# The last SwiGLU products of a feed-forward block are rounded into the end of another buffer

## What is computed

```python
def swiglu(x, w_gate, w_up, w_down):
    return (jax.nn.silu(x @ w_gate) * (x @ w_up)) @ w_down

h = h + 0.5 * swiglu(rmsnorm(h, ffn_norm_a[i]), ffn_a_w_gate[i], ffn_a_w_up[i], ffn_a_w_down[i])
m = rmsnorm(h, mix_norm[i])          # then the mixer, then a second such block
```

## Time and profile before

| | us |
|---|---|
| median of 3 executions | 1533.07 (1533.01 to 1557.75) |
| the profiled execution | 1533.33 |
| its span | 1531.5 |

### The profile page before, as it was taken

One profiled execution on the slowest core, in us unless ns is written; L12 is line 12 of the kernel. 1 busy time (PEld: TensorE's weight loads), 2 busy tenths in 40 slices (PEclk: granted clock), 3 DMA queues, 4 the chain that ended last, 5 costly groups with the idle time before them and its releaser, 6 DMA issues.

```text
span 1531.5 us, 24245 instructions
## 1 busy us (share of the span) xinstructions
PE 1448.1 (95%) x9470; PEld 1325.2 (87%) x9470; DVE 941.3 (61%) x1344; ACT 740.0 (48%) x1004; POOL 48.2 (3%) x88
## 2 busy tenths in 40 slices
PE   7999978899988999988999999999998999999997
PEld 7899978899987888888898888788887999888886
DVE  5545676655555665657756666666667369666655
ACT  5546553143435544435744544544444438554443
POOL 1000000000000000000010000100000000000000
PEclk9999989999999999979999999999999999999999
DMA  8342420155543555534156455475654410455552
GB/s 309 138 157 95 167 98 28 56 182 189 187 142 134 188 200 192 168 132 152 45 193 219 168 202 189 159 247 169 209 190 146 166 56 2 138 178 189 195 192 82
DMA packets 33907, 239.11 MB, mean 156 GB/s; under 512 B 3946, under 2 KB 4090, under 8 KB 5808
## 3 DMA queue, kind: packets, MB, share of 16 engines
q1 hardware_dynamic: 32544, 232.02, 43.9%
q0 software_dynamic: 1296, 6.15, 1.2%
HBM read 237.07 MB, written 1.08 MB: 156 GB/s over the span
## 4 chain that ended last, share of the span: by engine, by line
PE 79%; DVE 2%; ACT 1%; issue 1%; POOL 0%; POOLq 0%; DVEq 0%; ACTq 0%
PE ps L669 20%; PE ps L640 12%; PE ps L641 12%; PE ps L642 12%; PE ps L672 10%; PE ps L771 2%; PE ps L794 2%; PE ps L781 1%; PE ps L998 1%; PE ps L2191 1%; PE ps L2199 1%; PE ps L2203 1%; PE ps L582 1%; PE ps L2317 1%; PE ps L992 0%
## 5 line engine op out<-in xcount | busy, mean ns | idle before, releaser
L380 DVE TENSOR_TENSOR low<-raw,high 128x2048 fp32r<-128x2048 f32 (+1 forms) x193 | 437.8, 2268 | 252.5 <-ACT high L374 252.0
L374 ACT ACTIVATE high<-raw 128x2048 fp32r<-128x2048 f32 (+1 forms) x193 | 364.4, 1888 | 61.9 <-PE ps L642 56.5
L669 PE MATMUL ps<-nt,high 128*128 128x512 f32 x1344 | 335.8, 392 | 0.0
L669 PEld LDWEIGHTS ps<-nt,high 128*128 128x128 f32 x1344 | 244.2, 189 | 46.3 <-issue 0.9
L640 PE MATMUL ps<-nt,high 128*128 128x256 f32 x736 | 212.3, 288 | 6.4 <-DVE nt L471 5.5
L641 PE MATMUL ps<-nt,high 128*128 128x256 f32 x736 | 210.6, 286 | 0.0
L642 PE MATMUL ps<-nt,low 128*128 128x256 f32 x736 | 210.5, 286 | 0.0
L672 PEld LDWEIGHTS ps<-nt,low 128*128 128x128 f32 x1344 | 183.3, 190 | 13.1
L672 PE MATMUL ps<-nt,low 128*128 128x256 f32 x1344 | 187.4, 282 | 0.0
L640 PEld LDWEIGHTS ps<-nt,high 128*128 128x128 f32 x736 | 143.7, 195 | 7.9 <-DVE low L380 4.4
L640 PE MATMUL ps<-high,hth 128*128 128x512 f32 x352 | 138.0, 392 | 6.1 <-DVE htl L1173 6.1
(11 more groups left out here) (341 smaller groups left out, 2189.5 us busy)
## 6 DMA issues: line engine op xcount, KB each, us to landing
raw<-in_stream SPq DMA_DIRECT2D x217, 1024.0 KB, 4.9
late<-in_w POOLq DMA_DIRECT2D x1, 2048.0 KB, 8.7
scr<-bias_by_distance POOLq DMA_DIRECT2D x1, 2048.0 KB, 13.3
scr<-in_mem SPq DMA_DIRECT2D x2, 512.0 KB, 4.8
x<-in_x SPq DMA_DIRECT2D x1, 1024.0 KB, 8.8
out<-xs SPq DMA_DIRECT2D x2, 512.0 KB, 2.6
row<-in_row SPq DMA_DIRECT2D x1, 588.0 KB, 10.5
con<-in_con SPq DMA_DIRECT2D x1, 577.0 KB, 9.8
```

The lines of the kernel that those rows point to most:

```text
L374: nc.scalar.activation(high[t % SLOTS][:, 0:n], raw[t % SLOTS][:, 0:n], ACT.Copy).then_inc(w_high, 1)
L380: nc.vector.tensor_tensor(low[t % SLOTS][:, 0:n], raw[t % SLOTS][:, 0:n], high[t % SLOTS][:, 0:n].bitcast(F32), ALU.subtract).then_inc(w_l ...
L669: nc.tensor.matmul(r3(bank, 2), wt[0][:, k, col:col + P], nt[:, :, k, :], start=k == 0, stop=False, skip_group_check=True)
```

## The change

The high and low products of the last column of a block (c = 10) go into the last two chunks of `nth` and `ntl`, not into `hth` and `htl`. `last_down` reads them there. Since nobody reads these chunks any more, the rounding waits for the products alone and no longer for the ninth `down`. On ACT and DVE the last iteration of the loop is written out behind the loop, which now has eight; PE's loop keeps nine. In the written-out iteration the split of tile tb + 33 stands behind the rounding on ACT, and its low half behind the subtraction on DVE; before, both stood ahead of them.

```diff
+        hth_last, htl_last = nth[:, KC - 2:KC, :], ntl[:, KC - 2:KC, :]
@@ last_down
-                                             [h[:, j, P * tt:P * tt + P] for h in (hth, htl)],
+                                             [h[:, j, P * tt:P * tt + P] for h in (hth_last, htl_last)],
@@ act_ffn
-            with act.Fori(0, FT - 2) as i:
+            with act.Fori(0, FT - 3) as i:
                 split_high(act, tb + 7, i)
 ...
                 rounded(tb + 7, n0 + 2, i)
+            te, ne = tb + 3 * FT - 4, n0 + FT - 1
+            split_high(act, te + 2)
+            gate_cross(te, ne)
+            gated(ne)
+            split_high(act, te + 3)
+            up_cross(te + 1, ne)
+            act.wait_ge(ff_h, ne + 1)
+            nc.scalar.activation(hth_last, r3(ff["h"], 2), ACT.Copy).then_inc(ff_hhigh, 1)
+            split_high(act, te + 4)
@@ dve_ffn
-            with dve.Fori(0, FT - 2) as i:
+            with dve.Fori(0, FT - 3) as i:
                 split_low(dve, tb + 7, i)
 ...
                 rest(n0 + 2, i)
+            te, ne = tb + 3 * FT - 4, n0 + FT - 1
+            split_low(dve, te + 2)
+            gate_sum(ne)
+            gate_norm(ne)
+            split_low(dve, te + 3)
+            up_sum(ne)
+            hidden(ne)
+            dve.wait_ge(ff_hhigh, ne + 1)
+            nc.vector.tensor_tensor(htl_last, r3(ff["h"], 2), hth_last.bitcast(F32), ALU.subtract).then_inc(ff_hlow, 1)
+            split_low(dve, te + 4)
```

## The result

| | before | after |
|---|---|---|
| median of 6 executions each, us | 1533.23 (1533.01 to 1557.75) | 1556.23 (1555.75 to 1557.21) |
| ratio of the times, 95% interval | | 1.015 [1.0136, 1.0164] |
| span of the profiled execution, us | 1531.5 | 1554.4 |
| mean granted clock | 0.977 | 0.960 |

The kernel became slower by 23 us, where 1.4 us less was forecast and 1535.2 was the upper end. Each execution of either kernel is at one of two levels, about 24 us apart, and the ratio compares different ones: five of before at the lower, without its sixth at 1557.75, with all six of after at the upper.

What follows compares the result with a forecast made beforehand. PE was taken to bound the kernel, carrying 79% of the chain. Terms 0.37 + 0.42 + 0.64 - 1.8 + 1.77 gave 1.4 us less, 1531.7 us for the median, range 1529.3 to 1535.2.

Steps and rivals of the forecast that it cites:

- The rounding: End of each block: the low half is ready 1.1 us early, so PE saves 1.77 us if nothing else is late.
- Rival 4: The rounding is not in time, so the change does nothing: 1533.3 us; chance 0.04.
- DVE is late next; updates gain 0.42: Block ends: DVE must split two tiles before updating x, so updates, and block 1 with them, gain only 0.42 us.
- Blocks 0 and 2 gain 0.64: Norms behind these blocks: the second square follows the first directly, a gain of 0.64 us passed on to the turns.
- Idle stretches of 3.8 us: Behind blocks 0 and 2, PE's idle stretch ahead of the norm's turns grows from 2.48 to 3.8 us.
- The clock falls behind block 2, for 6.8 us, price 1.8: Behind block 2 the longer idle stretch brings half clock for 6.8 us, losing 1.8 us in turns and first products.
- Block 0, "0.37, if it comes back at the same moment": Behind block 0 the 0.64 us lead falls at half clock, worth 0.37 us if full clock returns at the same moment.
- the sum: Whole kernel: the gains and losses of blocks 0 to 3 and block 2's clock fall together give 1.4 us less.
- Rival 3: Block 0's half clock goes away because its stretch begins elsewhere: about 1525 us; chance 0.08.
- Rival 2: Half clock behind block 2 lasts long; at 17.0 us, 3.0 us slower, 1536.1; chance 0.17, mostly below 1535.

Runs made afterwards that it cites:

- late_low: The changed kernel with DVE's low half of tile +34 moved behind the updates and turned inputs: 1523.84 to 1525.16 us at full clock, 4 of 10 at half clock.
- after_again: The changed kernel run once more, nothing altered, beside before: ratio 0.9981 at full clock, 3 of 10 executions at half clock.
- before_late_norm: The kernel before, with ACT's first square of the norm behind block 0 made twice: ratio 1.0004, 10 of 10 at full clock.
- before_shift2: The kernel before, with two unused matmuls ahead of the first down of block 0: 1 of 10 at half clock, the others at ratio 1.0006.
- before_fill_all: The kernel before, with unused matmuls behind blocks 0 and 2, ahead of the latent inputs' turns and ahead of the attention's scores: 1530.5 us, ratio 0.9977.

## Why the prediction was right or wrong

Step by step, by distances from the last matmul of `up` of a block (L672), start to start, in the two traces:

- **The rounding.** Right. Block 3, where nothing is late next, ends 1.78 us earlier (end of its last product, 12.97 to 11.19); 1.77 was forecast. Rival 4 is out.
- **DVE is late next; updates gain 0.42.** Right: 0.45 in block 1 (first turn 11.26 to 10.81), and the new wait of 1.66 us for 1.5 forecast. late_low shows the cause: with the low half of +34 gone from ahead of the updates, the same distance is 8.99, another 1.8 us.
- **Blocks 0 and 2 gain 0.64.** Wrong by 0.2: the first turns come 0.46 and 0.45 earlier (15.47 to 15.01, 15.48 to 15.03). The second square did move as forecast (1187.85, right behind the first, 1.06 after it), but what follows did not gain by it: POOL's next step (L526) takes 0.65 us where it took 0.41, the one behind it (L529) starts 3.0 us after the first square in both kernels, and the second turns of block 2 stand 1.47 us behind the first in both.
- **Idle stretches of 3.8 us.** Right: 3.82 and 3.84.
- **The clock falls behind block 2, for 6.8 us, price 1.8.** Right in this trace. The fall is there and lasts 6.8 us (1190.48 to 1197.30). The first product comes 0.20 us closer behind `up` than before (19.32 to 19.12), but the products behind it are slower: the 41st stands 24.32 us behind `up` before (1175.50) and 25.53 after (1200.22), and all later ones keep this 1.21. With 0.45 gained ahead of the turns the fall costs 1.66, and block 2 loses 1.21 where the forecast, 0.64 less 1.8, was a loss of 1.16. How long the fall lasts is of the execution: in after_again it lies at 1165.39, lasts 3.4 us, and block 2 loses only 0.04 in all.
- **Block 0, "0.37, if it comes back at the same moment".** The condition failed. The half clock behind block 0 lasted 17.1 us before (663.55 to 680.62) and 20.5 after (661.41 to 681.89): it began 2.1 us earlier and ended 1.3 later. The first score came 0.7 us *later*, not 0.4 earlier (732.02 for 731.30), 0.51 of it behind block 0's last `up`. In after_again the half clock was 17.1 us again (663.63 to 680.69), with the same program, and the first score stood 0.17 closer behind `up` than before. So the moment of the fall belongs to the execution, not only to the kernel.
- **The places of the edit together.** In the trace of after they give -0.51 + 0.45 - 1.21 + 1.78 = 0.5 us less, for the 1.4 of the sum. The other side, 23.2 us more, is none of them.
- **The failing step** is a stage that the sum put at nothing: the attention behind block 0. The prediction followed the clock where the edit makes PE's idle stretches longer, behind blocks 0 and 2, and stopped there. The stretch of 2.16 us ahead of the attention is the same before and after, so it entered neither the sum, nor a rival, nor the range. Yet it is followed by a fall, and the work behind it can stay at half clock for 54.6 us. Rival 3's argument, that "all executions shown (1533.01, 1533.07 and the profiled 1533.33) agree too well for a fall that comes and goes", left out the fourth number in the table, 1557.75. That was by its time this very state, 24.7 us above the median (no trace of that execution was kept), and it said both that something in this kernel comes and goes and what it costs.
- **Rivals.** Rival 2 had the right sign and the right kind of mechanism at the wrong place: a half clock that lasts long. Its worst case, 17 us of products, was taken as the longest because the one trace showed none longer.

The Trainium skill, page "TensorE: Matmul & The Clock Gate", Part 1 (The HAM clock gate), says that the gate runs freely and does not restart with the kernel, so the same kernel meets it differently each time. The prediction quoted it, and bounded its effect by the edit's own places. The traces agree with the rule: ahead of all changed instructions, the fall near 210 us is at 209.58 in before and 209.66 in after_again, and at 210.85 in after. Had the rule been taken at its word, every stage behind an idle stretch would have been a candidate, the attention among them.

**At full clock over the attention** the change is worth 2.9 us by the medians (after_again), and 1.4 was forecast. The trace of after_again gives, place by place, 0.17 (first score) + 0.41 (first product of block 2) - 0.04 + 1.78 = 2.3 us, which is what its span is shorter by (1529.3 for 1531.5). The turns alone give more, 0.45 in each of blocks 0, 1 and 2, but the half clocks behind blocks 0 and 2 take 0.28 and 0.49 of that back. So the times of 1530.2 to 1531.5 at full clock, close to the 1531.7 of the forecast, do not confirm its sum: block 2's fall cost 0.49 there and not 1.8.

**What stays open.** Why the changed kernel was in the state more often (12 of 20 beside 9 of 52, and 3 of 4 with block 0 alone), and whether the change is the cause. For it: the share was higher in each of the three comparisons. Against it: in all five traces with the state the clock's course near 470 us was already another than in before, and nothing that the change touches had run. Executions of one kernel in a row may share that course by how they follow each other; no run tested this. In before, neither the length of the idle stretch behind block 0 (before_late_norm) nor a shift by two fills (before_shift2) brings the state. Traces with the state have the fall at least 1.07 us behind the first score and those without at most 0.70, but no run set this distance late on purpose. Before's own share differs from chip to chip, from 1 of 27 to 7 of 19, and nothing here says why. Shares from 4 to 10 executions are rough.

## What to carry to other kernels

Before an edit is costed, read the granted clock stage by stage, list each idle stretch of PE that is followed by a fall, touched by the edit or not, and price each stage behind one at both levels. An execution far from the others in the times of before is a price list: ask which stage it is before calling it noise. And a few unused matmuls in an idle stretch ahead of a stage of small matmuls, 0.47 us each (1.89 for four) in time that was idle, kept such a state away: none of 40 executions with them had it, so that small gains elsewhere could be kept and measured.

An execution's clock may be on another course before the edit's first instruction runs. So compare the granted clock ahead of the edit in the two traces first: where it differs already, a difference behind it is not yet the edit's.

## What the runs showed of the hardware that was not expected

- The half clock can last through work that keeps PE busy. Attention matmuls of 96x256, 128x128 and 128x64: 53.86 us busy in 54.5, clock 0.50 throughout; in before the same matmuls run at 1.00 for 39.4 us, once the clock has come back early.
- A fall can come behind a short idle stretch: in before_fill_all the longest in the 4 us ahead of 667.04 is 1.28 us, with PE busy 2.35 of 4.00 us. Then follow 13.5 us at 0.50 with PE busy 13.50. In this stretch a matmul of 128 columns takes as long as one of 256 (mean ns in the group rows):

```profile
L642 PE MATMUL ps<-high,nt 128*128 128x128 f32 x15 | 6.2, 414 | 0.0
...
L642 PE MATMUL ps<-nt,low 128*128 128x256 f32 x7 | 2.8, 405 | 0.0
```

- One program on one chip gives two times 1.5% apart. For before the share of the slower one ran from 1 of 27 to 7 of 19 over chips; beside it, kernels a few instructions away had it in 0 of 10 or in 3 of 4.
